# Score maps of seven forget heads: two 128-row products for four of 64 rows, with operands copied inside SBUF

## The reference

```python
c = jnp.cumsum(log_f, axis=-1)                     # (B,H,S) log forget gates, summed
sc = jnp.einsum('bhqd,bhkd->bhqk', qb, k) * scale  # scale = 1/sqrt(64)
sc = sc + (cb[..., :, None] - c[..., None, :])
sc = jnp.where(pos[None, :] <= tq[:, None], sc, NEG_INF)
p = jax.nn.softmax(sc, axis=-1)
out = jnp.einsum('bhqk,bhkd->bhqd', p, v)
```

## Time and profile before

| | |
|---|---|
| median of 3 runs | 1411.0 us (1410.42 to 1411.23) |
| profiled execution | 1412.2 us |
| its span | 1410.5 us |
| TensorE busy | 1368.1 us, 97% of the span |
| VectorE, ScalarE, GpSimd busy | 71%, 50%, 10% |
| forget heads of the second block | 800 to 932 us of the span |

### The profile page before, as it was taken

One profiled execution on the slowest core, in us unless ns is written; L12 is line 12 of the kernel. 1 busy time (PEld: TensorE's weight loads), 2 busy tenths in 40 slices (PEclk: granted clock), 3 DMA queues, 4 the chain that ended last, 5 costly groups with the idle time before them and its releaser, 6 DMA issues.

```text
span 1410.5 us, 19633 instructions
## 1 busy us (share of the span) xinstructions
PE 1368.1 (97%) x7774; PEld 1180.7 (84%) x7774; DVE 997.4 (71%) x1383; ACT 711.7 (50%) x1153; POOL 140.2 (10%) x115
## 2 busy tenths in 40 slices
PE   8999999999999999999999999999789999999997
PEld 6888888788679999978887788887568999998885
DVE  5799898786687878785337845667777787877332
ACT  4466886643465555562225434544345555555221
POOL 2188344100100000030000000000000000000000
PEclk9999999999999999999999999999899999999999
DMA  9422112466502323316431231110121233332321
GB/s 362 153 89 91 45 46 90 135 212 221 209 16 90 120 91 118 137 45 194 134 98 67 76 104 60 46 46 16 61 89 35 101 103 107 104 122 95 100 90 60
DMA packets 41131, 147.28 MB, mean 104 GB/s; under 512 B 4560, under 2 KB 4816, under 8 KB 40912
## 3 DMA queue, kind: packets, MB, share of 16 engines
q1 hardware_dynamic: 41040, 146.03, 30.5%
HBM read 143.91 MB, written 2.10 MB: 104 GB/s over the span
## 4 chain that ended last, share of the span: by engine, by line
PE 85%; DVE 9%; ACT 4%; issue 2%; DMA 0%; POOL 0%; DVEq 0%; SPq 0%; ACTq 0%; POOLq 0%
PE ps L1601 26%; PE ps L1602 26%; PE ps L1603 26%; PE ps L1744 1%; DVE t_buf L994 1%; DVE w_lo L960 1%; PE ps L1643 1%; DVE act_lo L1244 1%; PE ps L1983 1%; ACT w_hi L495 1%; PE ps L1970 1%; PE ps L1654 1%; PE ps L1655 1%; PE ps L1659 1%; DVE h_lo L986 1%
## 5 line engine op out<-in xcount | busy, mean ns | idle before, releaser
L1601 PE MATMUL ps<-h_hi,w_hi 128*128 128x256 f32 (+1 forms) x1120 | 375.3, 335 | 4.0 <-ACT sq L721 1.1
L1602 PE MATMUL ps<-h_lo,w_hi 128*128 128x256 f32 (+1 forms) x1120 | 372.2, 332 | 0.0
L1603 PE MATMUL ps<-h_hi,w_lo 128*128 128x256 f32 (+1 forms) x1120 | 372.1, 332 | 0.0
L960 DVE TENSOR_TENSOR w_lo<-raw,w_hi 128x1024 fp32r<-128x1024 f32 x141 | 182.8, 1300 | 113.0 <-ACT w_hi L495 112.3
L1601 PEld LDWEIGHTS ps<-h_hi,w_hi 128*128 128x128 f32 x1120 | 213.1, 190 | 30.2 <-issue 6.6
L1603 PEld LDWEIGHTS ps<-h_hi,w_lo 128*128 128x128 f32 x1120 | 213.2, 190 | 20.4
L1602 PEld LDWEIGHTS ps<-h_lo,w_hi 128*128 128x128 f32 x1120 | 213.3, 190 | 19.5 <-issue 0.5
L495 ACT ACTIVATE w_hi<-raw 128x1024 fp32r<-128x1024 f32 x141 | 148.1, 1055 | 146.3 <-PE ps L1603 77.5
L950 DVE TENSOR_TENSOR w_lo<-quads,w_hi 128x1024 fp32r<-128x1024 f32 (+1 forms) x152 | 164.7, 1085 | 72.8 <-ACT w_hi L495 72.8
L495 ACT ACTIVATE w_hi<-quads 128x1024 fp32r<-128x1024 f32 (+1 forms) x152 | 144.3, 949 | 78.5 <-PE ps L1603 76.8
L1601 PE MATMUL ps<-act_hi,w_hi 128*128 128x512 f32 x352 | 137.7, 391 | 2.2 <-DVE act_lo L1244 2.1
(11 more groups left out here) (290 smaller groups left out, 2270.3 us busy)
## 6 DMA issues: line engine op xcount, KB each, us to landing
quads<-in_ffn_in SPq DMA_DIRECT2D x76, 512.0 KB, 4.4
raw<-in_ffn_out SPq DMA_DIRECT2D x44, 512.0 KB, 3.7
raw<-in_ada SPq DMA_DIRECT2D x32, 512.0 KB, 4.2
raw<-in_qk SPq DMA_DIRECT2D x25, 512.0 KB, 3.7
ada<-in_ada SPq DMA_DIRECT2D x16, 512.0 KB, 9.6
raw<-in_gates SPq DMA_DIRECT2D x16, 512.0 KB, 3.6
raw<-in_v SPq DMA_DIRECT2D x12, 512.0 KB, 3.7
raw<-in_ffn_in SPq DMA_DIRECT2D x12, 512.0 KB, 3.8
```

The costliest lines, as they stand in the source:

```text
L960: nc.vector.tensor_tensor(w_lo[SLOT[p]][:], raw[q % RAW][:], w_hi[SLOT[p]][:].bitcast(f32), ALU.subtract).then_inc(raw_used, 1)
L1601: nc.tensor.matmul(out, w[0], v[0], start=start, stop=False, **kw)
L1602: nc.tensor.matmul(out, w[0], v[1], start=False, stop=False, **kw)
L1603: return nc.tensor.matmul(out, w[1], v[0], start=False, stop=stop, **kw)
```

## The change

For heads 1 to 7 the four products of a block become two of 128 rows. The first has the query's high half on both halves of the partitions against the key's high half above and its low half below: hi by hi and hi by lo at once. The second has the query's low half above and the rows of -1 below, against the key's high half above and the gate sums below: lo by hi and the gate term at once. Head 0 keeps its four products.

The operands are put together by DMA from SBUF to SBUF, issued from ScalarE's queue (`both_halves`). Once, for head 1: the lower half of `fc_hl` into `k_row` and the lower half of `sel[:, 0]` four times into `q_row`; ScalarE waits for these five to land. Then, for each head, six copies of 64 rows by 512 columns (128 KB) and two of one row (2 KB), which put the head's gate sums on rows 64 and 96, where `sel[:, 0]` has its -1. There is one set of operands, so the copies for head n wait for the map of head n-1. In ScalarE's order they stand ahead of `exps(0)` for head 1, behind `exps(1)` for head 2, and between `exps(h+2)` and `qk3_tile(h+1)` for head h+3. TensorE waits for them ahead of the first of the head's products, behind its mask products. `q_both`, `k_both` and `k_row` lie over `c_all` and `lam4`, `q_row` over `rstd`, which are not in use by then; the area behind them starts 1 KB later.

```diff
-        lam4 = place("lam4", [P, 4, HD], f32)
...
+        rstd_at = top[0]
         rstd = place("rstd", [P, SEQ], f32)
...
+        c_at = top[0]
         c_all = place("c_all", [P, D], f32)
+        lam4 = place("lam4", [P, 4, HD], f32)
+        top[0] = c_at + 6 * K
+        q_both, k_both, k_row = (place(n, [P, SEQ], f32r, at=c_at + 2 * K * i)
+                                 for i, n in enumerate(("q_both", "k_both", "k_row")))
+        q_row = place("q_row", [P, SEQ], f32r, at=rstd_at)
...
+            def both_halves(n):
+                rows, q_tile, k_tile = slice(HD * (n % 2), HD * (n % 2) + HD), n // 2, 4 + n // 2
+                upper, lower = slice(0, HD), slice(HD, P)
+                if n == 1:
+                    act.wait_ge(lo_of["qk2"], 5)
+                    act.wait_ge(fc_ready, 3)
+                    act.wait_ge(sel_ready, 3)
+                    nc.scalar.dma_start(k_row[lower, :].bitcast(f32), fc_hl[lower, :].bitcast(f32)).then_inc(both_in, 16)
+                    for b in range(NB):
+                        nc.scalar.dma_start(q_row[lower, P * b:P * (b + 1)].bitcast(f32), sel[lower, 0, :].bitcast(f32)).then_inc(both_in, 16)
+                    act.wait_ge(both_in, 16 * (1 + NB))
+                else:
+                    act.wait_ge(lo_of["qk2"], 8)
+                    act.wait_ge(s_done, NB * n)
+                for to, src, tile in ((q_both[upper, :], m_hi, q_tile), (q_both[lower, :], m_hi, q_tile),
+                                      (k_both[upper, :], m_hi, k_tile), (k_both[lower, :], m_lo, k_tile),
+                                      (q_row[upper, :], m_lo, q_tile), (k_row[upper, :], m_hi, k_tile)):
+                    nc.scalar.dma_start(to.bitcast(f32), src[rows, tile, :].bitcast(f32)).then_inc(both_in, 16)
+                for at in (HD, HD + 32):
+                    nc.scalar.dma_start(k_row[at:at + 1, :].bitcast(f32), fc_hl[at + n:at + n + 1, :].bitcast(f32)).then_inc(both_in, 16)
...
             prepare("v2", 0)
+            both_halves(1)
             exps(0)
...
             exps(1)
+            both_halves(2)
...
                 if h < HEADS - 2:
                     exps(h + 2)
+                    if h + 3 < HEADS:
+                        both_halves(h + 3)
                     qk3_tile(h + 1)
...
                     out = ps[:, bank, at:at + w]
+                    if 0 < n < HEADS:
+                        if qb == 0:
+                            pe.wait_ge(both_in, 16 * (1 + NB + 8 * n))
+                        nc.tensor.matmul(out, q_both[:, queries], k_both[:, 0:w], start=False, stop=False, **free)
+                        nc.tensor.matmul(out, q_row[:, queries], k_row[:, 0:w], start=False, stop=True, **free).then_inc(s_done, 1)
+                        continue
```

More of the change, by code:

```diff
@@ L272, in build @@
         lam_dot, lam_exp = sem("lam_dot"), sem("lam_exp")
+        both_in = sem("both_in")
         dn_sq, dn_ms, dn_eps, dn_rstd, dn_o, dn_norm, dn_hi, dn_ready = (
@@ L840, in exps @@
                                          accum_out=stat[:, n % 4, 1, qb:qb + 1]).then_inc(s_exp, 1)
+            def both_halves(n):
[7 more added lines that the diff above has]
+                    for b in range(NB):
+                        nc.scalar.dma_start(q_row[lower, P * b:P * (b + 1)].bitcast(f32), sel[lower, 0, :].bitcast(f32))                           .then_inc(both_in, 16)
+                    act.wait_ge(both_in, 16 * (1 + NB))
[7 more added lines that the diff above has]
+                for at in (HD, HD + 32):
+                    nc.scalar.dma_start(k_row[at:at + 1, :].bitcast(f32), fc_hl[at + n:at + n + 1, :].bitcast(f32))                       .then_inc(both_in, 16)
             def transposed(n):
@@ L1967, in softmax_scores @@
                     out = ps[:, bank, at:at + w]
+                    if 0 < n < HEADS:
+                        if qb == 0:
+                            pe.wait_ge(both_in, 16 * (1 + NB + 8 * n))
+                        nc.tensor.matmul(out, q_both[:, queries], k_both[:, 0:w], start=False, stop=False, **free)
+                        nc.tensor.matmul(out, q_row[:, queries], k_row[:, 0:w], start=False, stop=True, **free)\
+                            .then_inc(s_done, 1)
+                        continue
                     mul(out, (m_hi[rows, q_tile, queries], m_lo[rows, q_tile, queries]),
```

## The result

The changed kernel takes 1419.17 us (median of five runs, 1415.13 to 1420.19), the kernel before 1411.23 (1410.42 to 1413.03) beside it: 1.0050 times, 95% interval 1.0039 to 1.0061. It is 7.9 us slower where 8.5 us less were forecast, and above the range of 1400.0 to 1409.5. The profiled execution took 1419.2 us (span 1417.4).

What follows compares the result with a forecast made beforehand. TensorE was taken to bound the forget heads. Removed products (8.8) and switches (1.4) give 10.2 us, less 1.7 of waits for copies: 8.5 us gained, 1402.5 us, range 1400.0 to 1409.5.

Steps and rivals of the forecast that it cites:

- the pitch: ScalarE's queue: time p from one copy's issue to the next, taken as 0.42 us, between 0.37 and 0.475.
- F: Forget-head loop: end of the weighted sum, where the maps start; the last copy was forecast to land at F + 10.95.
- 12p - 4.8: Start of the stage: how late TensorE gets the last v panel, 0.25 us, with p the time per issue.
- early issue: ScalarE's sequencer issues copies while exponentials still execute, so issues in the loop start at F + 5.9.
- "slower" rival: ScalarE's cycle bounds the loop, with dearer issues: loss 52p - 16.8, for example 1415.4 us at 0.6; chance 0.12.
- The bound: Forget heads: TensorE is busy throughout, so a microsecond less of its work is a microsecond off the end.
- The steps of the products: Maps of heads 1 to 7: two of four products go at unchanged step, 1.26 us a head, 8.8 us.
- The switch out: First projection product behind a 64-row map takes 0.43 us, the next 0.23; the 0.20 goes, 1.4 us for seven.
- The landing in the loop: Copies of 128 KB land 2.1 us after issue, bounds 1.5 and 3.7.
- Waits for copies at every second head: TensorE stalls ahead of the map every second head only, about 1.7 us over heads 3 to 7.
- The switch in: First 64-row map product takes 0.25 us, the next 0.11; gain taken as 0, bounds 0 and 1.0 over seven heads.
- The start: Head 1's copies on ScalarE delay the last v panel by 0.25 us, which an earlier start of 1.0 hides.

Runs made afterwards that it cites:

- e1: Changed kernel with all 61 copies issued from SyncE in place of ScalarE; 1399.1 us, 0.9912 times the kernel before.
- e5: Changed kernel with the mask products of heads 3, 5 and 7 issued ten times; 1414.6 us, 1.0027 times the kernel before.
- e7: Changed kernel with head 1's copies from SyncE and, for other heads, four of eight from each queue; 1405.0 us, 0.9952 times the kernel before.
- e9: e1 plus a probe behind the last layer: SyncE issues SBUF copies and HBM loads of 64 and 128 rows; four 64-row issues take 2.43 us.
- e8: Changed kernel with copies for heads 2 to 7 from SyncE, head 1's still from ScalarE; 1406.0 us, 0.9964 times the kernel before.
- e2: Changed kernel with the copies kept on ScalarE but maps made with the old four products; 1417.6 us, 1.0039 times the kernel before.

## Why the prediction was wrong

**The step that failed first is the pitch.** "Pitch p is therefore 0.37 to 0.475 us" took its bounds from loads from HBM of full height, and allowed half of that for half the partitions; none of the issues in the earlier trace rows is of half the partitions or goes from SBUF to SBUF. Measured: an issue takes 0.62 us on ScalarE, one every 0.65. In the forecast's own formula for the last landing this is 5.9 + 7 x 0.65 + 2.1 = F + 12.55, 2.4 us late; three such waits are 7.2 us, which is what the trace after has. With 2.0 at the start (12p - 4.8 less the 1.0 of early issue) the forecast's sum would have been -10.2 + 7.2 + 2.0 = -1.0, a time of 1410.0. So the pitch accounts for 7.5 of the 16.4 us between forecast and result. Most of the rest is a term that the prediction did not have, the clock, below.

**A rival that came near by luck.** The "slower" rival names the place and breaks even at p = 0.52; by its formula, 52p - 16.8 at 0.65 is a loss of 17.0 against the 10.2, a time of 1417.8. That dearer issues on ScalarE cost more than the products give is what happened, in the loop and at the start, and its chance of 0.12 followed from the bounds on p. But the formula lets the issues begin only behind the exponentials, which the trace contradicts. In the loop it charges 14.0 us for ScalarE's cycle, where 7.2 of waiting and 5.4 of slow steps were measured, and at the start 3.0, where 4.3 and 1.8 were. That the sum comes within 1.4 us of the result is luck. (Its example, 1415.4 at p = 0.6, should read 1415.2.)

**Right.** The bound: 1 us of TensorE work less in this stage is 1 us off the end, as e1 shows. The steps of the products: 8.8. The switch out: 0.20 a head. Early issue: issues start about when the last exponential does, as forecast, and even so ScalarE's cycle is 11.5 to 11.9 (e5). The landing in the loop: 2.5 us for 128 KB (median; 2.2 to 3.8) and 1.8 for the last, 2 KB, against 2.1. Waits for copies at every second head: three, ahead of heads 3, 5 and 7, where the sum had its two longer waits at heads 4 and 6.

**The switch in.** Taken as 0 between bounds of 0 and 1.0 us; it is the whole 0.14 a head. It is not the change from the bf16 mask, which stays in e1, where the first product takes 0.12. The TensorE side is worth 11.2, the sum that the Trainium skill's rule gave.

**The start.** "... so 12p - 4.8 = 0.25 us late; with early issue an earlier start of 1.0 hides it". With p = 0.65 it is 3.0; the first five copies take 4.3 us from the last issue to landing, 2.2 more than counted; early issue hides 1.0. 3.0 + 2.2 - 1.0 = 4.2, measured 4.3. Of that, 0.7 is the issue itself: the last of the four took 1.34 us. Why is open, and so is the rest.

**The clock, the term that was missing.** It is not in the prediction at all, neither as a term nor as a rival, and is 7.2 us in the trace after. The wait at the start and each of the three in the loop (2.7 us at the longest) are followed by products at the 1.2 GHz level, 1.8 us each time. Of the loop's share some 3 us are real, by e5, since ScalarE's cycle covers the rest. Of the start's share: A is 6.2 us longer, 4.3 of waiting and 1.8 of slow steps.

**The sum by measured terms.** -11.2 (products and both switches) + 4.3 + 7.2 (waits, start and loop) + 7.2 (slow steps behind four waits) = +7.5 us, and A + B is 7.5 us longer than before. The medians differ by 7.9.

**The price of issuing.** The Trainium skill says that the time to initiate a DMA is usually small beside the transfer (DMA: Bandwidth & Descriptors, Issuing engines are not separate DMA queues). That misleads for these pieces: 0.62 us of sequencer stand beside 1.8 to 2.5 to landing, and eight issues take 5 us for 0.77 MB. In e1 the copies do cost nothing, since SyncE has the time.

**Open.** Why an issue on half the partitions, or from SBUF to SBUF, is dearer, and what in the issues ahead of it raises the price of a load. Why single issues take 1.3 to 2.0 us (one at 870.22 in the profile after, 1.97; also on SyncE, 1.31 at 836.35 in e7). What, beside the wait, decides that the clock falls. And the 0.8 to 1.1 us of e1's gain, by medians or by ratio, that lie outside A and B.

## What to carry to other kernels

Price the issue of a DMA by one of the same kind, source, number of partitions and place behind others; if the trace has none, measure it first, because eight of them on a busy engine can be worth more than the work they save. Small copies belong on a queue with nothing urgent behind them: moved from ScalarE to SyncE, the same 61 copies turn a loss of 0.5% into a gain of 0.9%, and e1 is the version to keep. And where a change turns a TensorE without gaps into one with waits, allow for slow products behind them: here 1.8 us behind most waits of 2.2 us or more.

## What the hardware showed that was not expected

- Right behind another issue a piece of 64 rows costs 0.60 to 0.62 us of the issuing queue, on SyncE and ScalarE, from SBUF or HBM; behind such pieces a single row or 64 rows by 128 columns cost as much (e1, after). The first of a group costs 0.46 to 0.54.
- Copies of 128 rows inside SBUF cost 0.47 to 0.50 and 0.60 behind another, loads of 128 rows from HBM 0.33 and 0.43 (e9), but 0.58 right behind eight copies of the other kind (e1).
- ScalarE's queue issues while its activations still execute: two issues overlap the last exponential (892.47 and 893.01 beside 892.72 to 893.41).
- The granted clock fell to 0.50 to 0.66 of full behind waits of 2.2 to 4.3 us, not behind waits of 0.9 to 1.3 us (e5, e7), and in one trace (e8) not behind 3.5 us. Behind the wait of 0.8 us at the head of the stage it fell in e2 and e8 and in no other of these traces.
- A change of the products' height costs 0.20 us out of the 64-row map and 0.14 us into it.
